# Two halves of tokens through the norms of a transformer block's second part, in place of one pass with filler products

## The reference, cut to what matters

```
for mixer or ffn, weights w_pre, w_post:           # four times
    h = rms_norm(x, w_pre)                          # 1024 features, eps 1e-6
    y = mixer_or_ffn(h)                             # ends in a product with 1024 x K weights
    x = x + rms_norm(y, w_post)
out = x[16:]                                        # after the fourth, without the 16 tokens
```

## Time and profile before

| what | value |
| --- | --- |
| runs | 2646.14, 2652.50, 2653.24 us; median 2652.5 us |
| the profiled execution | 2646.19 us, its span 2644.4 us |
| mean granted TensorE clock | 0.977 of 2.4 GHz |
| busy | TensorE 94%, weight loads 83%, VectorE 51%, ScalarE 37%, GpSimd 36% |

### The profile page before, as it was taken

The page is one execution under the profiler, slowest core; times in us unless marked ns, Lnnn a source line. Parts: engine busy times, 40 slices in busy tenths (PEclk is TensorE's granted clock), DMA queues, the critical chain, the costliest instruction groups (busy, mean ns, idle before and its releaser), DMA issues.

```text
span 2644.4 us, 44454 instructions
## 1 busy us (share of the span) xinstructions
PE 2493.2 (94%) x19232; PEld 2207.1 (83%) x19232; DVE 1353.1 (51%) x2061; ACT 973.9 (37%) x1558; POOL 954.4 (36%) x549
## 2 busy tenths in 40 slices
PE   7989977999999999999999999999998988999997
PEld 5877766788887878878999999988988977989896
DVE  4646576653534544454364444466654535645453
ACT  5234543332223433424433333354333233333332
POOL 1755342344445212212445454500002214454544
PEclk9999998999999999999999999999999998999998
DMA  8432212333333211111223232312111012232321
GB/s 249 131 106 73 80 31 67 101 96 92 93 94 96 57 41 49 41 44 39 79 75 109 81 97 84 89 49 64 42 34 37 18 33 61 81 105 87 104 80 57
DMA packets 379858, 201.26 MB, mean 76 GB/s; under 512 B 6400, under 2 KB 377088, under 8 KB 379664
## 3 DMA queue, kind: packets, MB, share of 16 engines
q1 hardware_dynamic: 379664, 198.42, 26.5%
HBM read 196.30 MB, written 2.10 MB: 75 GB/s over the span
## 4 chain that ended last, share of the span: by engine, by line
PE 61%; DVE 12%; ACT 5%; issue 2%; POOL 1%; POOLq 0%; ACTq 0%; DVEq 0%
PE ps L677 48%; DVE t_ffy L2934 3%; DVE t_atq L2728 2%; ACT t_wh L645 1%; PE ps L2536 1%; PE ps L3169 1%; PE ps L2509 1%; DVE t_ffy L2937 1%; PE ps L2475 1%; PE ps L3188 1%; ACT t_ffy L2837 1%; PE ps L3192 1%; DVE t_ainv L2756 1%; DVE t_wl L655 1%; PE ps L519 1%
## 5 line engine op out<-in xcount | busy, mean ns | idle before, releaser
L655 POOL TENSOR_TENSOR t_wl<-t_raw,t_wh 128x1024 fp32r<-128x1024 f32 (+2 forms) x196 | 443.6, 2264 | 803.9 <-ACT t_wh L645 803.8
L677 PE MATMUL ps<-t_hh,t_wh 128*128 128x264 f32 (+2 forms) x1712 | 403.0, 314 | 11.3 <-DVE t_dcq L2662 3.6
L645 ACT ACTIVATE t_wh<-t_raw 128x1024 fp32r<-128x1024 f32 (+2 forms) x253 | 255.5, 1012 | 416.6 <-PE ps L677 374.2
L677 PE MATMUL ps<-t_hh,t_wl 128*128 128x264 f32 (+2 forms) x1712 | 379.3, 300 | 6.2 <-POOL t_wl L655 3.1
L677 PE MATMUL ps<-t_hl,t_wh 128*128 128x264 f32 (+2 forms) x1712 | 376.2, 301 | 0.0
L677 PEld LDWEIGHTS ps<-t_hh,t_wh 128*128 128x128 f32 x1712 | 269.9, 191 | 36.0 <-issue 19.8
L677 PEld LDWEIGHTS ps<-t_hh,t_wl 128*128 128x128 f32 x1712 | 270.0, 190 | 22.8 <-issue 6.3
L677 PEld LDWEIGHTS ps<-t_hl,t_wh 128*128 128x128 f32 x1712 | 269.1, 191 | 14.6 <-issue 7.1
L2934 DVE SCALAR_TENSOR_TENSOR t_ffy<-t_ffp,t_vec,t_ffy 128x528 f32<-128x528 f32 (+1 forms) x88 | 176.5, 2005 | 179.0 <-ACT t_ffy L2837 179.0
L655 POOL TENSOR_TENSOR t_fwl<-t_raw,t_fwh 128x1024 fp32r<-128x1024 f32 (+1 forms) x72 | 167.9, 2333 | 153.5 <-ACT t_fwh L645 153.5
L677 PE MATMUL ps<-t_fhh,t_wl 128*128 128x512 f32 (+1 forms) x704 | 210.9, 340 | 2.9 <-POOL t_wl L655 2.8
(11 more groups left out here) (571 smaller groups left out, 5431.3 us busy)
## 6 DMA issues: line engine op xcount, KB each, us to landing
t_raw<-in_up SPq DMA_DIRECT2D x44, 512.0 KB, 3.8
t_raw<-in_up2a SPq DMA_DIRECT2D x44, 512.0 KB, 3.8
t_raw<-in_up2b SPq DMA_DIRECT2D x44, 512.0 KB, 3.9
t_raw<-in_attn_in SPq DMA_DIRECT2D x33, 512.0 KB, 4.2
t_raw<-in_dn_in SPq DMA_DIRECT2D x33, 512.0 KB, 4.1
t_raw<-in_ada_w SPq DMA_DIRECT2D x32, 512.0 KB, 4.2
t_raw<-in_w_in SPq DMA_DIRECT2D x25, 512.0 KB, 4.1
t_raw<-in_down SPq DMA_DIRECT2D x16, 512.0 KB, 4.0
```

The costliest lines, as they stand in the source:

```text
L645: ac.activation(wh[slot_of[j]][:, 0:kc, :], raw[r % NRAW][:, 0:kc, :], ACT.Copy).then_inc(up("wh_cut", "cut", j), 1)
L655: eng.tensor_tensor(wl[slot_of[j]][:, 0:kc, :], raw[r % NRAW][:, 0:kc, :], wh[slot_of[j]][:, 0:kc, :].bitcast(F), SUB).then_inc(up(name, " ...
L677: ins = pe.matmul(ps[bank_of(j, i)][:, 0:tn], wt[slot][:, k, :], a[:, k, t0:t0 + tn], start=first, stop=last)
```

## The change

The last panels before each of the four norms are taken out of the usual loop (`HALVED`: the last three of "ao", "down2" and "down3", the last two of "do") and run by `end_by_sides`: first all of them for side 0 of the tokens, then all of them for side 1. `SIDES` are 264 + 264, for the third norm 272 + 256, for the fourth 256 + 256 (where the panels were 512 wide before). Each half has its own `take_h`, `square_h` (square on ScalarE, sum on VectorE) and its own root and spread. The next three lead panels are run by `fed_by_sides`, all of side 0 before side 1, the third panel two chunks behind. The filler products (`put_busy` in `post_root`) are gone; the function `busy` stays for the first block. Roots take equal slices (528 = 6 x 88) in place of tiles of 128 and a rest. Some tiles lie at other addresses, so that panels 212 ("qkv"), 261 and 262 ("up3") may be cut earlier; `lev_load` and `gst_zero` wait for the last "down2" panel's products in place of the norm. The norm of the first block's end (q = 0) keeps its form.

```diff
-            if j in THIRD or slot_of[j] > 3 and slot_free[j] is None and p.stage != "ao":
-                slot_free[j] = max(i for i in range(j) if panels[i].stage != p.stage and i not in FED)
+                if p.stage == "up3":
+                    slot_free[j] = first_of("do", 1)
+                elif panels[j].stage == "gate" or THIRD[0] == j:
...
+                else:
+                    slot_free[j] = end_of("up2", 2) - 1
...
+        def slices_of(n):
+            k = next(k for k in range(-(-n // 128), n) if n % k == 0)
+            return [(t, n // k) for t in range(0, n, n // k)]
...
+        SIDES = {1: HALF, 2: HALF, 3: [(0, 272), (272, 256)], 4: [(NM, 256), (NM + 256, 256)]}
+        ENDS = {1: ("ao", 0, 3), 2: ("down2", 2, 3), 3: ("do", 1, 2), 4: ("down3", 2, 3)}
+        HALVED = {}
...
+        def put_high(a, c, i):
+            put("high", a, c, i)
+            if c == 4:
+                put("rows", a, 0, i, use=[side_banks[a][1 - i]])
+            put("rowsq", a, c, i)
+
+        def fed_by_sides(js, a):
+            for i in range(2):
+                for c in range(KD + 2):
+                    if c < KD:
+                        if i or c >= early_x[a]:
+                            put_x(a, c, i)
+                            put_high(a, c, i)
+                        for j in js[:2]:
+                            put("mm", j, c, 0, i)
+                            put("mm", j, c, 2, i)
+                    if c >= 2:
+                        put("mm", js[2], c - 2, 0, i)
+                        put("mm", js[2], c - 2, 2, i)
+                    if i == 0 and c == 5:
+                        put_roots(POST[a][1], side_banks[a][0:1])
+                if i == 0:
+                    put_spread(POST[a][1], side_banks[a][0:1])
+                for c in range(KD):
+                    put("low", a, c, i)
+                for c in range(KD):
+                    for j in js[:3]:
+                        put("mm", j, c, 1, i)
...
+                    if c == 2:
+                        put("rows", a, 1, i, use=[side_banks[a][1 - i]])
+                        sig.mark("copied", "rows", a, i)
+                    if i and c == 2 and slot_of[js[3]] > 3:
+                        cut_to(js[3], js[0])
+                    if i and c == 4:
+                        PRE[a] = root_of(L, ssum, ("copied", "rows", a, 1), 1.0 / D, rstd,
+                                         [("step_x", "x", a, KD - 1, 1, "a")])
+                        put_roots(PRE[a], side_banks[a][0:1])
+                    if i and c == KD - 1:
+                        put_spread(PRE[a], side_banks[a])
...
-        def post_root(q):
-            POST[q] = root_of(L - FROM[q], ssum, ("sq_dve", "square", POST[q][0], KD - 1), 1.0 / D, rstd)
-            last = q == 4
-            if not last:
-                put_busy(POST[q], 0, 4)
-            put_roots(POST[q])
-            if not last:
-                put_busy(POST[q], 1, 1)
-            put_spread(POST[q])
-            if not last:
-                put_busy(POST[q], 2, 6)
+        def end_by_sides(q):
+            stage, group, n = ENDS[q]
+            js = [j for j, x in HALVED.items() if x == q]
+            cut_to(js[-1], js[0])
+            flush()
+            put("warm")
...
+            for i in range(2):
+                t0, tn = side(q, i)
+                for x, j in enumerate(js):
+                    for k in range(panels[j].kc):
+                        for m in range(3):
+                            put("mm", j, k, m, i)
+                        if i and x == 1 and k == panels[j].kc // 2 - 1:
+                            put_spread(POST[q][0], side_banks[q][0:1])
...
+                    put("take_h", j, i)
...
+                    early = n == 3 and i and x == 1
+                    if early:
+                        put_x(q, 0, 0)
+                    put_square_h(q, c, i)
+                    if early:
+                        for c in range(3 if panels[j].kc > 6 else 2):
+                            if c:
+                                put_x(q, c, 0)
+                            if q < 4:
+                                put_high(q, c, 0)
+                        early_x[q] = c + 1
+                    if i and x == 0:
+                        put_roots(POST[q][0], side_banks[q][0:1])
+                    done = js[0] - 1 if i == 0 else j
+                    while q < 4 and state["cut"] < js[-1] + 4 and slot_free[state["cut"]] <= done:
+                        cut_to(state["cut"], j)
...
-        for c in range(KD):
-            put_x(4, c)
-        for c0 in range(0, KD, 4):
-            for i in range(4):
-                put("turn_out", c0, i, banks=1, of=8)
+        for c in range(early_x[4], KD):
+            put_x(4, c, 0)
+            if c == 4:
+                put_roots(POST[4][1], side_banks[4][0:1])
+                put_turn(0, 0)
+                put_turn(0, 1)
+        put_spread(POST[4][1], side_banks[4][0:1])
+        put_turn(4, 0)
+        put_turn(4, 1)
+        for c in range(KD):
+            put_x(4, c, 1)
+            if c % 4 == 3:
+                put_turn(c - 3, 2)
+                put_turn(c - 3, 3)
```

More of the change, by code:

```diff
@@ L383, in gemm @@
         def gemm(stages, then=None, keep=1, every=0, feed=None, tail=False, group=0, two=False, until=None,
-                 done=0, pair=None):
-            js = [j for j, p in enumerate(panels) if p.stage in stages and p.group == group]
+                 done=0, pair=None, sides=None):
+            js = [j for j, p in enumerate(panels) if p.stage in stages and p.group == group and j not in HALVED]
             if pair is not None:
@@ L422, in gemm @@
                         cut_to(js[3], js[0])
+                cut_to(js[3], js[0])
+                for j in js[:3]:
+                    taken(j, then, keep=keep)
+                kept.clear()
+                begin = 3
+            elif sides:
+                cut_to(js[2], js[0])
+                kept.update(bank_of(js[2], i) for i in range(2))
+                fed_by_sides(js, sides)
                 cut_to(js[3], js[0])
@@ L671, in mm @@
                 if n == 0 and j in FED:
-                    w.wait_ge(s.hi_set, at("hi_set", "high", feed_at[j], k))
+                    w.wait_ge(s.hi_set, at("hi_set", "high", feed_at[j], k, *half))
+                elif j in FED and half and n == 1:
+                    w.wait_ge(s.lo_dve, at("lo_dve", "low", feed_at[j], k, *half))
                 elif n == (1 if j in FED else 0):
@@ L1974, in program @@
         sb_ = ExitStack()
+        with ExitStack() as st:
+            sbt(st, "dqpre", [128, 2, L])
+            third = [sbt(st, f"dw3{i}", [128, 2, L], R) for i in range(2)]
         dq = sbt(sb_, "dq", [128, 8, L])
-        with ExitStack() as st:
-            third = [sbt(st, f"dw3{i}", [128, 2, L], R) for i in range(2)]
         ogT = sbt(sb_, "dog", [128, 8, L])
@@ L2072, in post_sums, with side, feed_first2 @@
-        def post_sums(q, stage, group):
+                sig.mark("step_x", "x", q, c, *i, "a")
+            e = x_done(q, c, *i)
+            sig.mark(*e)
+        def side(a, *i):
+            return SIDES[a][i[0]] if i else (0, L)
+        def feed_first2(what, c):
+            if what == "high":
+                put_x(0, c)
+                put("high", 0, c)
+                if c == 0:
+                    rows_hold[0] = list(sqb_last)
+                if c == 4:
+                    put("rows", 0, 0, banks=2)
+                put("rowsq", 0, c)
+            elif what == "low":
+                put("low", 0, c)
+            elif c == 2:
+                put("rows", 0, 1)
+                banks_at["rows", 0, 1] = bank("rows", 0, 0)
+                sig.mark("copied", "rows", 0)
+                sqb_last[:] = [("summed", "rows", 0, 1)] * 2
+            elif c == 4:
+                PRE[0] = root_of(L, ssum, ("copied", "rows", 0), 1.0 / D, rstd, [("step_x", "x", 0, KD - 1)])
+                put_roots(PRE[0])
+            elif c == KD - 1:
+                put_spread(PRE[0])
@@ L2092, in program @@
         SIGNALS.update({
-            "high": "hi_set", "low": "lo_dve", "rowsq": "squared", "rows": "summed", "ffn_zero": "pool_x",
+            "high": "hi_set", "square_h": "squared sq_dve", "low": "lo_dve", "rowsq": "squared", "rows": "summed", "ffn_zero": "pool_x",
             "uconv0": "copied conved act_fn", "uconv1": "copied conved normed hi_set lo_pool",
```

313 lines of the change are left out of this document (188 added, 125 removed).

## The result

The changed kernel takes 2662.15 us (median of five runs, 2660.51 to 2662.62) against 2652.5 us for the kernel before beside it: ratio 1.0037, interval [1.0026, 1.0049]. It is slower, by 0.4%. The forecast was 2640 us, with 0.07 for slower by over 0.3%.

What follows compares the result with a forecast made beforehand. TensorE, busy 94%, was taken as the bound. Savings at the norms of 1.0 + 2.2 + 2.7 + 6.7 = 12.6 us took the profiled 2646.19 us to 2633.6; allowing for the higher median, the forecast was 2640, range 2628 to 2650.

Steps and rivals of the forecast that it cites:

- the four holes: TensorE without real products at norms 1 (after "ao"), 2 ("down2"), 3 ("do"), 4 ("down3"): 58.1 us, 2.2% of the span.
- Norm 1's low part at T1 + 4.8: Third lead panel's low weights ready 4.8 us after T1, the new end of the last product; TensorE idle 3.2 us.
- GpSimd's cut in norm 1 and the memsets in norm 2: Expected releasers of idle TensorE: GpSimd's cut in norms 1 and 3, ScalarE's "high" behind the memsets in norm 2.
- The rest: Moved memsets and table load nothing, six root slices under 1 us, SBUF addresses 0, between -1 and +1.
- it catches up during the same idle time: Norm 1: VectorE, going on only at T1 + 3.1, catches up while TensorE idles 3.2 us for the low part.
- half 1's root as 0.6 us of TensorE: In each lead, a half's root costs TensorE 0.6 us, with its spread 0.75 more, 1.35 us together.
- the forecast of the leads: Lead products behind norms 1, 2 and 3 save 1.0, 2.2 and 2.7 us.
- The idle terms: TensorE waiting in the leads of norms 1, 2 and 3: 3.2, 3.7 and 5.1 us.
- The clock: Loss from TensorE falling to 1.2 GHz after idling in norms 1, 2 and 3: 2.2, 2.1 and 1.2 us.
- The tail: Norm 4, last product to the end: 20.0 us against 26.75, 6.7 us saved; bounds 9 and 4.
- The only slower one: Rival: without fillers the clock stays at 1.2 GHz; all three leads make 25 us slower, 2677; chance 0.07.
- The one about VectorE's fixed costs: Rival: 0.15 us fixed per VectorE instruction loses 8.6 us in three leads; only tail gained, 4 us faster, 2648; chance 0.15.

Runs made afterwards that it cites:

- r11: r7 with norm 1's third-panel cut again behind the early high operands and norm 2's memsets again ahead of the lead; 2645.32 us, 0.9981 of before.
- r4: The changed kernel with nothing halved and the filler products back; 2648.46 us, 0.9995 of before.
- r2: The changed kernel with the lead panels' low cuts on VectorE in place of GpSimd; 2661.16 us, 1.0039 of before.
- r6: The changed kernel with half 1's root behind all steps x, norm 1's cut and last sum moved, norm 2's memsets behind the lead's steps; 2644.66 us, 0.9981 of before.
- r7: r6 with the lead panels' low cuts on VectorE in place of GpSimd; 2640.18 us, 0.9957 of before.
- r10: r9 with half 1's root and spread earlier in the last norm and the second output tiles later; 2637.67 us, 0.9949 of before.
- r9: r7 with two steps x of half 0 ahead of the two weight cuts at norm 3; 2637.83 us, 0.9951 of before.

## Why the prediction was wrong

**Right.** The places of the four holes. Norm 1's low part at T1 + 4.8: 4.9. GpSimd's cut in norm 1 and the memsets in norm 2 as what ends a wait; r11 prices the two at 4.3 and 2.7 us, clock included. A pair of half steps at 0.88 us: 0.88. "The rest" at nothing: r4. In norm 3 the releaser was wrong: GpSimd's cut ends 0.30 us of the idle time, ScalarE's high operands end the other 3.36 and 2.78.

**Wrong, first step: "it catches up during the same idle time".** Each VectorE operation was priced as if alone. GpSimd's low cut beside it blocks one for its whole length: 2.36, 2.48, 2.60 and 2.47 us in place of 0.43 to 0.49. It stands ahead of the 1.32 us wait in norm 1, of the first wait of norm 2 (2.23 us) and of the 2.78 us of norm 3. Of these last, part would have been there anyway: the third panel's low part landed only at 2245.26, 0.9 us before that wait ended. Taking the blocking away alone (r2) gained nothing; with the queue order mended (r6 to r7) it gained 5.9 us over the three leads. Rows of before had shown it: I read VectorE's 1.63 us beside GpSimd in the tail and did not carry it to the leads.

**Wrong, second step: half 1's root as 0.6 us of TensorE.** It was counted as matmuls and not as a round trip TensorE, ScalarE, VectorE in the middle of three queues. It costs 1.95 to 1.98 us idle in each lead, and in norm 1 a second fall of the clock; moving it gave 7.5 us in three leads. With it the forecast of the leads, +5.9 us of gain, would have been a small loss by itself.

**Mis-sized: idle time and clock.** The idle terms were 3.2, 3.7 and 5.1 us; TensorE idled 5.8, 7.5 and 8.4 in the three leads. The clock was 2.2, 2.1 and 1.2 us, for one fall per lead. Norm 1 has two: the 5.47 us at 0.50 hold 18 products and 8 matmuls of the row sums, which at the full clock are 18 x 0.122 + 0.52 = 2.7 us, so 2.8 lost; the 4.56 us at 0.63 hold 24 matmuls, 4.56 - 24 x 0.122 = 1.6 us lost. Norm 1 in all, beyond the ideal: idle 5.8 us (forecast 3.2) and, as an estimate, clock 4.4 (2.2). That is 4.8 us of the 6.4 between +1.0 and -5.4; the rest, some 1.6 us, is spread over the passes and not resolved. In norm 2 the idle time explains 3.8 of the 5.5 us between +2.2 and -3.3, in norm 3 3.3 of the 7.2 between +2.7 and -4.5; there too the rest is clock and what is not resolved.

**The tail** gained 4.2 or 3.3 us (norm 4 takes 34.9 or 35.8 in kernels whose tail is the same), at or under the lower bound given there, 4. The term missed is the turn between halves, 2.05 us idle (2.92 where the transposes ahead of it ran at 0.50) and a 0.69 us copy; r10 takes them away, meets another wait of VectorE for an output tile (1.45 us), and gains only 0.7.

**The rivals.** None was it. The only slower one needed a clock that stays at 1.2 GHz; it comes back to 1.00 in every lead. The one about VectorE's fixed costs had the right engine and the wrong reason. The base was also high: four later medians of before are 2649.2 to 2650.7, not 2652.5.

The idea itself was sound: r7's three leads are 2.7, 4.0 and -0.1 us shorter than before, 6.6 in all, where the forecast for the changed kernel was 5.9. Norm 3 gained nothing, and by the clock alone it can differ by 1.4 us (38.90 and 40.29 above). r7, r9 and r10, at 0.9949 to 0.9957, beat both kernels.

## What to carry to other kernels

Splitting a stage to overlap it with the next also splits every small round trip between engines. For each, write down its place in all the queues that it passes, not only its busy time: one reciprocal of 0.17 us between two steps left VectorE idle for 4 to 5 us ahead of it in each lead, and TensorE for 2 behind it. And price VectorE with GpSimd beside it; but expect nothing from mending a resource (r2) before the queue order that hides it is mended (r7).

## What the runs showed that was not expected

VectorE and GpSimd do not slow each other in proportion: here the one that came second waited for the whole of the other's instruction. Five times (the fifth is the 2.50 us of r6) VectorE's operation began while a low cut ran and ended 0.29 to 0.30 us behind it. The Trainium skill (SBUF — State Buffer, "SBUF: two separate sides") says that the pair of ports the two share is "an exclusive lock, not a bandwidth split", held for a whole instruction by whichever starts first, and that VectorE's operations with two SBUF inputs need it against a GpSimd operation that reads SBUF. The trace agrees: the sum, x's product and x's addition, all with two SBUF inputs, are those that took 2.4 to 2.6 us, and the addition with one input in PSUM kept its 0.42 us beside the cut at 2237.00.

A short wait need not cost clock, and an earlier start need not gain. In r7's norm 1 waits of 1.35 and 0.34 us left the clock at 1.00; in the changed kernel 0.51, 2.03 and 1.32 us were followed by 5.47 us at 0.50. In r9 a start 2.5 us earlier gave all of it back in a second wait (1.13 us) and at half clock (7.3 us).

A change can also go with another clock far from where it was made: with 24 fillers ahead of norm 1's lead, the 473.3 us of the mixer, 440 us later and unchanged, became 477.3 (one profile of each).
